# The four norms of a diffusion backbone: scale and shift move from VectorE's products to a ScalarE step of its own

## The reference, cut to what matters

```python
def _rmsnorm(x, w):
    xf = x.astype(jnp.float32)
    y = xf * lax.rsqrt(jnp.mean(xf * xf, axis=-1, keepdims=True) + NORM_EPS)
    return (y * w.astype(jnp.float32)).astype(x.dtype)

def _modulate(h, shift, scale):
    return h * (1 + scale) + shift
...
        h = _modulate(_rmsnorm(x, norm1_w[i]), sh1, sc1)
        hc = _modulate(_rmsnorm(ctx, norm1_w[i]), csh1, csc1)
...
        h2 = _modulate(_rmsnorm(x, norm2_w[i]), sh2, sc2)
```

## Time and profile before

| what | us |
|---|---|
| median of three runs | 2104.57 |
| lowest, highest | 2098.45, 2106.68 |
| the profiled execution | 2100.11 |
| its span | 2098.2 |
| PE busy | 1994.6 (95%) |
| DVE busy | 1336.1 (64%) |
| ACT busy | 749.5 (36%) |
| from the spread root to the first matmul on h, norm 2 | 746.46 to 750.18 |
| the same, norm 3 | 1320.79 to 1324.80 |
| the same, norm 4 | 1712.41 to 1714.94 |

### The profile page before, as it was taken

One profiled execution on the slowest core, in us unless ns is written; L12 is line 12 of the kernel. 1 busy time (PEld: TensorE's weight loads), 2 busy tenths in 40 slices (PEclk: granted clock), 3 DMA queues, 4 the chain that ended last, 5 costly groups with the idle time before them and its releaser, 6 DMA issues.

```text
span 2098.2 us, 30012 instructions
## 1 busy us (share of the span) xinstructions
PE 1994.6 (95%) x10500; PEld 1702.0 (81%) x10500; DVE 1336.1 (64%) x2241; ACT 749.5 (36%) x1274; POOL 97.4 (5%) x162
## 2 busy tenths in 40 slices
PE   5989999999999989999999999799999789999997
PEld 5778888888888868888888888688888668888885
DVE  5665735635745677766664567777877557557476
ACT  3333223313313343412331233456556335324242
POOL 0000000000000000000000000211111000000000
PEclk9999999999999989999999999899999899999998
DMA  7221221221221112233224324211111212222222
GB/s 278 71 90 61 100 71 61 82 91 61 79 93 61 61 41 100 92 128 120 90 90 132 108 95 152 102 46 41 55 45 35 81 61 100 100 97 93 97 93 101
DMA packets 50762, 186.40 MB, mean 89 GB/s; under 512 B 5569, under 2 KB 5569, under 8 KB 50561
## 3 DMA queue, kind: packets, MB, share of 16 engines
q1 hardware_dynamic: 37248, 136.73, 18.9%
q0 software_dynamic: 13440, 48.63, 6.9%
HBM read 181.15 MB, written 4.19 MB: 88 GB/s over the span
## 4 chain that ended last, share of the span: by engine, by line
PE 84%; DVE 7%; issue 4%; ACT 3%; DMA 1%; DVEq 0%; SPq 0%; ACTq 0%
PE acc L383 58%; PE o_ps L469 4%; PE o_ps L500 3%; PE acc L469 3%; PE acc L588 3%; PE o_ps L631 2%; PE acc L646 2%; PE acc L487 2%; PE acc L434 2%; PE o_ps L646 2%; DVE pt_lo L1548 1%; DMA x<-in_x_in_dram 1%; PE acc L621 1%; PE o_ps L420 1%; ACT w_hi L779 1%
## 5 line engine op out<-in xcount | busy, mean ns | idle before, releaser
L779 ACT ACTIVATE w_hi<-raw 128x1024 fp32r<-128x1024 f32 x232 | 245.1, 1057 | 615.3 <-PE acc L383 498.2
L1125 DVE TENSOR_TENSOR w_lo<-raw,w_hi 128x1024 fp32r<-128x1024 f32 x232 | 284.0, 1224 | 272.6 <-ACT w_hi L779 271.1
L383 PE MATMUL acc<-h_hi,w_hi 128*128 128x512 f32 x1520 | 434.6, 349 | 4.6 <-DVE w_lo L1125 3.4
L383 PE MATMUL acc<-h_lo,w_hi 128*128 128x512 f32 x1520 | 434.4, 349 | 0.0
L383 PE MATMUL acc<-h_hi,w_lo 128*128 128x512 f32 x1520 | 434.3, 349 | 0.0
L383 PEld LDWEIGHTS acc<-h_hi,w_hi 128*128 128x128 f32 x1520 | 244.0, 188 | 45.7 <-ACT u L942 4.2
L383 PEld LDWEIGHTS acc<-h_hi,w_lo 128*128 128x128 f32 x1520 | 243.9, 188 | 39.3
L383 PEld LDWEIGHTS acc<-h_lo,w_hi 128*128 128x128 f32 x1520 | 243.2, 188 | 38.9
L1253 DVE SCALAR_TENSOR_TENSOR x<-acc,mod,x 128x512 f32<-128x512 f32 (+3 forms) x136 | 81.9, 636 | 144.9 <-PE acc L383 136.0
L383 PE MATMUL acc<-act_hi,w_lo 128*128 128x512 f32 (+1 forms) x396 | 119.7, 356 | 0.0
L383 PE MATMUL acc<-act_lo,w_hi 128*128 128x512 f32 (+1 forms) x396 | 119.6, 356 | 0.0
(11 more groups left out here) (224 smaller groups left out, 3536.9 us busy)
## 6 DMA issues: line engine op xcount, KB each, us to landing
raw<-in_weights_dram SPq DMA_DIRECT2D x232, 512.0 KB, 3.3
ada_raw<-in_ada_dram POOLq DMA_DIRECT2D x80, 512.0 KB, 3.5
ada_start<-in_ada_first_dram SPq DMA_DIRECT2D x4, 2048.0 KB, 22.4
x<-in_x_in_dram SPq DMA_DIRECT2D x1, 3072.0 KB, 23.5
park_dram<-x POOLq DMA_DIRECT2D x1, 2048.0 KB, 8.1
rel<-in_bias_dram POOLq DMA_DIRECT2D x16, 128.0 KB, 2.4
out_dram<-x SPq DMA_DIRECT2D x8, 256.0 KB, 2.1
x<-park_dram POOLq DMA_DIRECT2D x1, 1536.0 KB, 9.1
```

What stands on the lines that cost most here:

```text
L383: mm = nc.tensor.matmul(tile[:, c0:c0 + cn], wt[:, b * P:(b + 1) * P], mv[:, n, c0:c0 + cn], start=(n == 0 and m == 0), stop=(n == last an ...
L779: nc.scalar.activation(w_hi[i][:, :], raw[i][:, :], ACT.Copy).then_inc(hi_split, 1)
L1125: nc.vector.tensor_tensor(w_lo[i][:, :], raw[i][:, :], w_hi[i][:, :].bitcast(F32), ALU.subtract)\
```

## The change

VectorE's first product loses its `norm_a` factor and takes all columns in one instruction, except in norm 3, where the reordering keeps the two ranges apart. ScalarE gets two steps in place of one. The first applies `norm_a` as its scale and the shift as its bias and writes the full value of h to `S[k % 2]`. The second waits for the first and rounds that to `h_hi`, all columns in one instruction. VectorE's rest becomes a plain subtraction of two tensors, again in one instruction. A new semaphore, `h_made`, stands between ScalarE's two steps, and from chunk 2 on ScalarE waits for `h_lo_done` of the chunk two before, which frees the buffer `S[k % 2]`. Since all four calls go through the same function, all four norms are changed.

```diff
@@ ScalarE, norm
                     act.wait_ge(norm_t, normed.up())
+                    if k >= 2:
+                        act.wait_ge(h_lo_done, normed.now() - 2)
                     for c0, cn, c in parts:
-                        ins = nc.scalar.activation(h_hi[:, k, c0:c0 + cn], S[2 + k % 2][:, c0:c0 + cn], ACT.Identity,
-                                                   bias=mod[:, layer, shift + k, c:c + 1])
-                    ins.then_inc(h_hi_done, 1)
+                        ins = nc.scalar.activation(S[k % 2][:, c0:c0 + cn], S[2 + k % 2][:, c0:c0 + cn], ACT.Identity,
+                                                   scale=norm_a[:, k, c:c + 1], bias=mod[:, layer, shift + k, c:c + 1])
+                    ins.then_inc(h_made, 1)
+                    act.wait_ge(h_made, normed.now())
+                    nc.scalar.activation(h_hi[:, k, 0:width], S[k % 2][:, 0:width], ACT.Copy).then_inc(h_hi_done, 1)
@@ VectorE, norm
-                    for c0, cn, c in parts:
+                    for c0, cn, c in (parts if by_column else ((0, width, 0),)):
                         o, a, b = (z[:, c0:c0 + cn] for z in (S[2 + k % 2], x[:, k, :], spread))
...
-                        ins = nc.vector.scalar_tensor_tensor(o, a, norm_a[:, k, c:c + 1], b, ALU.mult, ALU.mult)
+                        ins = nc.vector.tensor_tensor(o, a, b, ALU.mult)
...
-                    for c0, cn, c in parts:
-                        ins = nc.vector.scalar_tensor_tensor(h_lo[:, k, c0:c0 + cn], S[2 + k % 2][:, c0:c0 + cn],
-                                                             mod[:, layer, shift + k, c:c + 1],
-                                                             h_hi[:, k, c0:c0 + cn].bitcast(F32), ALU.add, ALU.subtract)
-                    ins.then_inc(h_lo_done, 1)
+                    nc.vector.tensor_tensor(h_lo[:, k, 0:width], S[k % 2][:, 0:width], h_hi[:, k, 0:width].bitcast(F32),
+                                            ALU.subtract).then_inc(h_lo_done, 1)
```

More of the change, by code:

```diff
@@ L232, in backbone @@
         sums_done, root_done, diag_done, spread_done = sem("sums_done"), sem("root_done"), sem("diag_done"), sem("spread_done")
-        norm_t, h_hi_done, h_lo_done = sem("norm_t"), sem("h_hi_done"), sem("h_lo_done")
+        norm_t, h_made, h_hi_done, h_lo_done = sem("norm_t"), sem("h_made"), sem("h_hi_done"), sem("h_lo_done")
         dist_ready, decay_exp = sem("dist_ready"), sem("decay_exp")
```

## The result

| | before | after |
|---|---|---|
| median of 20 runs each | 2103.89 | 2112.81 |
| lowest to highest | 2098.45 to 2112.91 | 2105.55 to 2118.48 |
| span of the profiled execution | 2098.2 | 2109.1 |
| ratio after / before | | 1.0039, 95% interval 1.0028 to 1.0049 |

The forecast was 2107.2 with a range of 2099 to 2112. The change costs 8 to 9 us where 2.6 had been summed.

The account below looks back on a forecast made before the run. TensorE matmuls fill 95% of the span; each norm's chunk 0 is paid in full. Norms 0.72 + 0.72 + 0.49 + 0.68 = +2.6 us on the median 2104.57 gave 2107.2, range 2099 to 2112.

Parts of the forecast that it names:

- The first chunk: Chunk 0 of each norm, paid in full before TensorE starts: +0.72, +0.72, +0.90 and +0.68 us.
- ScalarE's two column operands: ScalarE's first step with scale and shift as columns: 1.29 us instead of 1.13 for 512 + 256 columns.
- The own wait: ScalarE's rounding waits until its own first step has written: 0.11 us, bounds 0 and 0.2.
- Later chunks: Chunks 1 to 7 of each norm: ScalarE's pace 2.2 us, covered by TensorE; norm 3 loses a 0.41 us wait.
- The clock rivals: TensorE's half-clock stretch after each norm's wait changes the cost: takes half (chance 0.22) or takes more (0.12).
- takes more: Rival: TensorE's half-clock stretch grows in norms 1, 3 and 4; +5.4 us, 2110.0; chance 0.12.
- takes half: Rival: later starts are paid out of TensorE's half-speed matmuls, so half of 2.6: +1.3 us, 2105.9; chance 0.22.
- ScalarE as the bound: Rival: ScalarE's own wait and rounding outlast TensorE's cover in the norms; +10.0 us at x = 0.5; chance 0.04.
- x: Extra us per chunk of ScalarE's own wait and rounding above the forecast; above 0.1 lies outside all bounds.
- VectorE's saving ... ends nothing: VectorE's saving in the norms' chunks, some 9 us of its busy time, was claimed to shorten nothing.
- then something outside the norms has shifted: Sign of being wrong: the time moves over 10 us.
- what I don't see: Rival: something unseen, at either side, place and size not given; chance 0.06.

Follow-up runs that it names:

- the old places: Changed kernel with 40 one-column memsets on VectorE (16, 16, 8), or 4 behind norm 3, their tensor above all others: 1.0008 and 1.0010 of before.
- with 88 twice: Kernel before plus 88 one-column memsets at VectorE's start: 1.0044 with their tensor below the stage tensors, 1.0034 with it above all others.
- with 80: Kernel before plus 80 one-column memsets at VectorE's start: 1.0040 of before.
- with the tensor: Kernel before plus one unused tensor of 96 bytes per partition below the stage tensors, no instruction more: 1.0016 of before.
- the place alone: Kernel before plus 88 one-column memsets at VectorE's start, their tensor above all others: 1.0034 of before, 7.2 us.

## Why the prediction was wrong

**The first chunk** (+0.72, +0.72, +0.90, +0.68) was right: +0.66, +0.68, +0.76, +0.64. ScalarE's two column operands cost 1.31 against 1.29 forecast. The own wait, taken as 0.11 from the earlier trace rows, measured 0.02 to 0.04: between its bounds, but mis-sized by 0.08, which is more than the difference at the starts of norms 1, 2 and 4 (0.04 to 0.06). In norm 3 another 0.08 comes from the strided scaling, 1.33 where I had 1.41. With two inputs the stride still costs: its 512 columns alone take 1.13 on average, the dense 512 of norm 4 0.69.

**Later chunks** were right. ScalarE's pace is 2.1 (2.2 forecast), and TensorE waits for no chunk, not in norm 3 either, where 0.41 us of waiting has gone: the trace after has one wait of TensorE for h_lo there, the one for chunk 0. Net for the starts +2.3 where 2.6 was summed. The runs with the old places measure 1.7 and 2.1, with intervals that reach from -1 to +5.

**The clock rivals** can be judged from all traces together. I take the time from the end of the spreading to a later point of TensorE's chain, behind the half-clock stretch: in norm 1 the start of its seventh piece on "PE acc L469", in the others the end of the L434 pieces, 90 or 45 matmuls. Means over the five kernels with the norms of before (the kernel before, with 88 twice, with 80, with the tensor) and the seven traces with the changed norms:

| norm | norms of before | changed norms | difference | difference at the start |
|---|---|---|---|---|
| 1 | 30.4 | 31.5 | +1.1 | +0.66 |
| 2 | 22.2 | 22.4 | +0.2 | +0.68 |
| 3 | 22.9 | 22.8 | -0.2 | +0.76, less 0.41 |
| 4 | 15.2 | 16.0 | +0.9 | +0.64 |

The sum is +2.0 us. The sums of single traces reach from 89.9 to 91.3 with the norms of before and from 91.4 to 93.5 with the changed ones, so the difference is known to about 0.8 us either way: "takes more" (+5.4) is excluded, "takes half" (+1.3) and the forecast (+2.6) are not told apart. The slow stretch differs between traces of one kernel: the piece in norm 2 took 17.16 and 18.19 us in the two traces of the changed kernel, the first piece of norm 1 5.46 and 4.63. (In norm 1 the view gives the granted clock of these two traces as 1.00, though the first matmuls start 0.43 us apart and the later ones 0.23, so there it is read from the matmuls.)

**ScalarE as the bound** did not come: own wait and rounding cost less than summed, so x was below 0.

**The step that failed** is a term of the sum put at nothing: "VectorE's saving ... ends nothing", and with it that what lies outside the norms stays as it is. What it left out measured 7.2 us (the place alone), against 1.7 to 2.1 for all that was summed. I priced the 40 instructions that go by their duration, and found nothing that waits for them. But each also holds a place in the stream, and everything behind it moves up. The order of instructions showed it beforehand: it gives VectorE's attention loop from row 895 on in one kernel and from 855 in the other. The page showed that instructions are fetched by DMA at all, and the trace that turns two and three fetched nothing, so there was a state to lose. None of it has a price in a trace of a kernel where the loop happens to fit. The text's last clause named the case ("then something outside the norms has shifted") and gave it no chance beyond 0.06 for what I don't see. The range ended 0.8 us too low.

The Trainium skill describes the mechanism ("Runtime: NRT & Kernel Launch", Instruction fetch mechanics): instructions are prefetched strictly in sequence into a small window, and a taken branch whose target lies outside it forces a fetch before the engine goes on. The traces agree in this: gaps of 1.3 to 1.5 us on VectorE at the jump and within 2 us of it, with transfers in the same stretch. The Trainium skill gives blocks of 16 KiB in the same section; 29 transfers with 0.24 MB are 8 KB each on the queue concerned, and the measurement decides. That this queue serves VectorE's fetches is inferred: its transfers come and go with VectorE's gaps.

What stays open: why one body fits at one place and not at another (which blocks are kept when the engine jumps), how wide the bad stretch is, and why its price is 3.2 us at one place and 7.5 eight places further on.

## What to carry to other kernels

An edit that adds or removes instructions ahead of a long loop also moves the loop in its engine's instruction stream, and this can cost more than the edit: here 7 us against 2. Look at the turns of a loop one by one: if the first part of each later turn is slow, VectorE shows "issue" gaps in the middle of a program line, and instruction transfers stand beside them, the place is the first suspect, not the edit. Before judging such a change, run it once with fillers that put the loop back, and put what the fillers write where it moves no other tensor.

## What I had not expected

- A VectorE loop of 281 instructions costs nothing or 3 to 7.5 us over three turns, by its place alone. Four instructions more cure it: 29 transfers become 19, 41.7 and 43.3 us become 38.7.
- An unused tensor of 96 bytes per partition below the stage tensors costs 0.16% (1.0003 to 1.0029). The stretches between the groups of the last FFN go from 55.7 to 56.6 us; in the first FFN, groups two and three take 16.96 us a turn in all six kernels that have it there, where group two takes 16.64 in all seven traces without it. That it is the addresses is shown, through which mechanism is not.
- The same kernel takes 16.64 or 16.95 us a turn in groups one and three of the first FFN from one execution to the next, whole groups at a time. This accounts for about 6 us between two executions.
- A wait of ScalarE on its own previous instruction costs 0.02 to 0.04 us.
